# Three norms' reciprocal roots moved behind the projections, and RWKV's fills and transpositions moved, in a two-block hybrid kernel

## What is computed

```python
def rms_norm_2(x, g):
    y = xf * lax.rsqrt(jnp.mean(xf * xf, axis=-1, keepdims=True) + RMS_EPS)
    return (y * g.astype(jnp.float32)).astype(x.dtype)

def swiglu(h, w_gate, w_up, w_down):
    return (jax.nn.silu(h @ w_gate) * (h @ w_up)) @ w_down

h = h + 0.5 * swiglu(rms_norm_2(h, ffn1_norm), ffn1_w_gate, ffn1_w_up, ffn1_w_down)   # d_ff 2816
proj = rms_norm_2(h, mix_norm) @ w_in
sb_out = stick_breaking_attention(q, k, v)     # from the first 1536 columns of proj
rw_out = rwkv7_time_mix(proj[..., 1536:], ...) # shift, decays, a recurrence, group norm
h = h + concat([sb_out, rw_out]) @ w_out
h = h + 0.5 * swiglu(rms_norm_2(h, ffn2_norm), ffn2_w_gate, ffn2_w_up, ffn2_w_down)
out = rms_norm_2(h, final_norm)[:, 16:]
```

## Time and profile before

| | |
|---|---|
| median of 3 runs | 1085.91 us (1084.17 to 1086.17) |
| profiled execution | 1086.47 us, its span 1084.7 us |
| PE busy | 1000.6 us, 92% of the span |
| weight loads (PEld) | 952.5 us, 88% |
| DVE busy | 533.3 us, 49% |
| ACT busy | 535.3 us, 49% |
| POOL busy | 654.5 us, 60% |
| DMA | 139.79 MB, mean 129 GB/s |
| mean granted PE clock | 0.965 of 2.4 GHz |

### The profile page before, as it was taken

The page is one execution under the profiler, slowest core; times in us unless marked ns, Lnnn a source line. Parts: engine busy times, 40 slices in busy tenths (PEclk is TensorE's granted clock), DMA queues, the critical chain, the costliest instruction groups (busy, mean ns, idle before and its releaser), DMA issues.

```text
span 1084.7 us, 22914 instructions
## 1 busy us (share of the span) xinstructions
PE 1000.6 (92%) x9068; PEld 952.5 (88%) x9068; DVE 533.3 (49%) x735; ACT 535.3 (49%) x765; POOL 654.5 (60%) x271
## 2 busy tenths in 40 slices
PE   5997999898799778999999999999999989999996
PEld 5986778697799766899999998999898979999996
DVE  4335433554410895586652003474363668777301
ACT  5565555466554445644444446666321454444441
POOL 2784233356689830698787875554620169888882
PEclk8998999989899899999999999999898999999999
DMA  8552122133355200455555554333200036555551
GB/s 320 191 167 87 61 75 94 63 126 124 127 187 174 79 1 1 140 191 175 179 170 176 173 175 136 117 117 98 98 4 2 21 135 195 194 185 182 188 181 41
DMA packets 38993, 139.79 MB, mean 129 GB/s; under 512 B 4224, under 2 KB 5504, under 8 KB 38784
## 3 DMA queue, kind: packets, MB, share of 16 engines
q1 hardware_dynamic: 38912, 138.62, 37.8%
HBM read 137.55 MB, written 1.05 MB: 128 GB/s over the span
## 4 chain that ended last, share of the span: by engine, by line
PE 55%; issue 22%; POOL 12%; DVE 8%; ACT 2%; DMA 1%; SPq 0%; POOLq 0%; DVEq 0%; ACTq 0%
PE ps L667 55%; POOL wlo L602 11%; DVE qkl L1834 3%; DVE hA L2133 1%; DVE hT L1866 1%; ACT whi L1463 1%; ACT dif L1402 1%; DMA ring<-in_stream 1%; DVE sq L1834 0%; ACT rstd L1402 0%; PE ps L1208 0%; POOL dif L626 0%; DVE hA L1834 0%; DVE rGI L1834 0%; DVE aL L1872 0%
## 5 line engine op out<-in xcount | busy, mean ns | idle before, releaser
L602 POOL TENSOR_TENSOR wlo<-ring,whi 128x1024 fp32r<-128x1024 f32 x251 | 611.5, 2453 | 381.4 <-ACT whi L1463 380.3
L667 PE MATMUL ps<-aH,whi 128*128 128x256 f32 (+1 forms) x1528 | 445.4, 291 | 27.1 <-DVE aL L1834 10.3
L667 PE MATMUL ps<-aH,wlo 128*128 128x256 f32 (+1 forms) x1528 | 439.7, 288 | 0.0
L667 PE MATMUL ps<-aL,whi 128*128 128x256 f32 (+1 forms) x1528 | 439.5, 288 | 0.0
L1463 ACT ACTIVATE whi<-ring 128x1024 fp32r<-128x1024 f32 x253 | 266.4, 1058 | 123.7 <-PE ps L667 108.0
L667 PEld LDWEIGHTS ps<-aH,whi 128*128 128x128 f32 x1528 | 294.8, 193 | 35.8 <-issue 17.7
L667 PEld LDWEIGHTS ps<-aH,wlo 128*128 128x128 f32 x1528 | 294.8, 193 | 0.0
L667 PEld LDWEIGHTS ps<-aL,whi 128*128 128x128 f32 x1528 | 294.2, 193 | 0.3 <-issue 0.2
L667 PE MATMUL ps<-fH,wlo 128*128 128x272 f32 (+1 forms) x352 | 100.8, 286 | 0.0
L667 PE MATMUL ps<-fH,whi 128*128 128x272 f32 (+1 forms) x352 | 100.4, 285 | 0.0
L667 PE MATMUL ps<-fL,whi 128*128 128x272 f32 (+1 forms) x352 | 100.4, 285 | 0.0
(11 more groups left out here) (336 smaller groups left out, 1303.4 us busy)
## 6 DMA issues: line engine op xcount, KB each, us to landing
ring<-in_stream SPq DMA_DIRECT2D x253, 512.0 KB, 3.3
cst<-in_cst SPq DMA_DIRECT2D x1, 1325.0 KB, 13.4
xT<-in_x SPq DMA_DIRECT2D x4, 272.0 KB, 3.5
out<-hT SPq DMA_DIRECT2D x1, 1024.0 KB, 4.6
row<-in_row SPq DMA_DIRECT2D x1, 898.0 KB, 9.9
cst<-in_cst SPq DMA_DIRECT2D x1, 640.0 KB, 10.9
mat<-in_mat SPq DMA_DIRECT2D x1, 576.0 KB, 14.2
vec<-in_vec SPq DMA_DIRECT2D x1, 135.0 KB, 3.8
```

Source lines behind the costliest of these rows:

```text
L602: nc.gpsimd.tensor_tensor(wlo[:, s, :], ring[:, s, :], whi[:, s, :].bitcast(F32), ALU.subtract).then_inc(S("w_split"), 1)
L667: return nc.tensor.matmul(out, lhsT, rhs, start=start, stop=stop, skip_group_check=True)
```

## The change

**Norms of ffn1, mix and ffn2 (`LATE`).** The activations of the next projection are now `xT` times the gain, without `rstd`: as soon as a tile of `xT` is there, ACT writes the high part and the square, and DVE the low part (`low_half`), within `residual`. For the FFNs they lie in `fxH` and `fxL`, which share the memory of `hT` and `mixT`. PE starts the projection's first pair and only behind it makes the norm sum, one matmul, for which DVE adds all eight squares. No filler stands at these norms any more, and the copy of the last weight ahead is made before `rstd` on ACT. `rstd` is applied behind the projection: in the FFN, DVE multiplies the gate's bank in place and ACT's tanh waits for that (`ffn_gate`); the up half needs it also, so the result of the down projection is multiplied in `residual` (tags mix and final). In the mixer, DVE multiplies each RWKV tile in place ahead of ACT's shift (`mix_scaled`) and drains q, k and v itself with the multiply in the same step (before: ACT).

**RWKV.** POOL's `inverse_starts` now comes before the `wlo` of the first four units of the output projection, which follow it. The key transpositions, four before at one place behind the ladder, now stand one behind the last level, two ahead of the second group's last products, one where it was, in other banks.

```diff
+LATE = ("ffn1", "mix", "ffn2")
+SUMMED = {n: 8 if n in LATE else 5 for n in NORMS}
...
-            lows(U_HO + SLOTS, U_PO + SLOTS)
+            lows(U_HO + SLOTS, U_PO)
             inverse_starts()
-            lows(U_PO + SLOTS, N_UNITS)
+            lows(U_PO, N_UNITS)
...
             def norm(tag, n):                                       # PE
-                else:
+                elif tag not in LATE:
                     filler(1)
-                pe.wait_ge(S("norm_sum"), (SUMMED - 1) * (i + 1))
-                mm(ps[:, 7, 0:n], C("ones"), sq[:, 0, 0:n], True, False)
+                pe.wait_ge(S("norm_sum"), sums_up_to(tag))
+                m = mm(ps[:, 7, 0:n], C("ones"), sq[:, 0, 0:n], True, SUMMED[tag] == KT)
...
-                if i and tag != "final":
+                if tag == "norm1":
                     filler(3)
...
-                feature_pair(u0, g0, c0, ("norm_h", NORMS.index(tag) * KT))
+                feature_pair(u0, g0, c0, ("norm_h", NORMS.index(tag) * KT), tag)
+                norm(tag, TT - c0)
...
-                pe.wait_ge(S("drained_a"), drained("a", G_P + 11 + 3 * m))
+                pe.wait_ge(S("drained_v"), drained("v", G_P + 11 + 3 * m))
...
+                turned(6, key(0, 0)).then_inc(S("r_tok"), 1)
                 pe.wait_ge(S("r_wc"), 3)
                 for g, b in ((0, 0), (1, 4)):
                     pe.wait_ge(S("r_g"), level_count(last_level(g), g))
+                    if g == 1:
+                        turned(2, key(0, 1)).then_inc(S("r_tok"), 1)
+                        turned(3, key(1, 0)).then_inc(S("r_tok"), 1)
...
-                turned(2, key(0, 0)).then_inc(S("r_tok"), 1)
-                turned(3, key(0, 1)).then_inc(S("r_tok"), 1)
-                turned(6, key(1, 0)).then_inc(S("r_tok"), 1)
                 pe.wait_ge(S("r_tokb"), 1)
-                turned(2, key(1, 1)).then_inc(S("r_tok"), 1)
+                turned(6, key(1, 1)).then_inc(S("r_tok"), 1)
...
+                if tag in LATE:                                      # ACT, square()
+                    func(acts(tag)[0][:, k, c0:TT], xT[:, k, c0:TT], ACT.Identity, "norm_hi", scale=V(tag, k))
                 func(sq[:, k, 0:n], xT[:, k, c0:c0 + n], ACT.Square, "norm_sq")
...
+                if tag in LATE:                                      # ACT, squares_behind()
+                    ahead(u0 + n_units - 1)
                 norm(tag, n)
-                ahead(u0 + n_units - 1)
+                if tag not in LATE:
+                    ahead(u0 + n_units - 1)
...
-                    act.wait_ge(S("w_used"), it * 8 + (u0 + 2 * f4 + 1))
+                    act.wait_ge(S("ffn_gate"), it * 4 + (first + f4 + 1))
...
             def residual(tag, g0, c0, scale=1.0):                    # DVE
+                for m in range(KT + 1):
+                    if m < KT:
+                        dve.wait_ge(S("w_used"), used_by(g0 + m))
+                        if tag in ("mix", "final"):
+                            tt(out, out, rstd[:, 0:TT - c0], ALU.mult)
+                        stt(xT[:, m, c0:TT], out, scale, xT[:, m, c0:TT], ALU.mult, ALU.add, "drained_v")
+                    if tag in LATE and m >= 1:
+                        low_half(tag, m - 1, wide)
+                if tag in LATE:
+                    for k in range(1, SUMMED[tag]):
+                        add_square(tag, k, wide)
+                    dve.wait_ge(S("norm_rstd"), NORMS.index(tag) + 1)
+
+            def low_half(tag, k, n):
+                high, low = [t[:, k, TT - n:TT] for t in acts(tag)]
+                dve.wait_ge(S("norm_hi"), NORMS.index(tag) * KT + k + 1)
+                stt(low, xT[:, k, TT - n:TT], V(tag, k), high.bitcast(F32), ALU.mult, ALU.subtract, "norm_h")
...
+                    gate = ps[:, (g0 + 2 * f4) % MM_BANKS, 0:TT - c0]   # DVE, pair()
+                    dve.wait_ge(S("w_used"), it * 8 + (u0 + 2 * f4 + 1))
+                    nc.vector.tensor_tensor(gate, gate, rstd[:, 0:TT - c0], ALU.mult).then_inc(S("ffn_gate"), 1)
                     dve.wait_ge(S("ffn_th"), it * 4 + (first + f4 + 1))
...
+                    if i is None:                                    # DVE, mixer_in()
+                        kind, m = P_STICK[j]
+                        stt(stick[kind][:, m, 0:TT], now, 0.125 if kind == "q" else 1.0, rstd[:], ALU.mult, ALU.mult, "drained_v")
+                    else:
+                        tt(now, now, rstd[:], ALU.mult, "mix_scaled")
                         dve.wait_ge(S("shift"), n_shift + 1)
...
-            norm("ffn1", 0, TT, "ffn1")
             ffn(U_F1, G_F1, 0, 0)
-            norm("mix", 0, TT, "mix")
```

More of the change, by code:

```diff
@@ L77 @@
 P_STICK = [None] * 10 + [(n, j) for j in range(4) for n in "qkv"] + [None] * 4
-P_OWNER = "".join("a" if t is None else "v" for t in P_RWKV)
+P_OWNER = "v" * 26
 P_Z = {12: 0, 15: 1, 18: 2, 21: 3}
@@ L91 @@
 MM_BANKS = 4
-SUMMED = 5
 def chunk_bank(c):
@@ L360, with sums_up_to @@
 NORMS = ("norm0", "norm1", "ffn1", "mix", "ffn2", "final")
+LATE = ("ffn1", "mix", "ffn2")
+SUMMED = {n: 8 if n in LATE else 5 for n in NORMS}
+def sums_up_to(tag):
+    return sum(SUMMED[n] - 1 for n in NORMS[:NORMS.index(tag) + 1])
 def used_by(g):
@@ L407, in program @@
         xT = sb("xT", [P, KT, TT])
-        hT = sb("hT", [P, KT, TT])
-        mixT = sb("mixT", [P, KT, TT])
+        own = ExitStack()
+        hT = sb("hT", [P, KT, TT], at=own)
+        mixT = sb("mixT", [P, KT, TT], at=own)
+        own.close()
+        fxH = sb("fxH", [P, KT, TT], F32R)
+        fxL = sb("fxL", [P, KT, TT], F32R)
         sq = sb("sq", [P, KT, TT])
@@ L539, in program, with acts @@
         mx.close()
+        def acts(tag):
+            return (fxH[:], fxL[:]) if tag in ("ffn1", "ffn2") else (aH[:], aL[:])
         def V(name, i=0):
@@ L1085, in mixer_in @@
                 feature_pair(U_P, G_P, 0, ("norm_h", 3 * KT))
+                norm("mix", TT)
                 for j in range(2, P_UNITS):
@@ L1415, in norm @@
                 func(rstd[:, 0:n], rstd[:, 0:n], ACT.Exp, "norm_rstd", scale=-0.5)
-                if tag != "final":
+                if tag in ("norm0", "norm1"):
                     for k in range(KT):
@@ L1723, in mixer_in @@
                            14: decay_products, 15: decay_quotients, 17: decay_inverses}
-                stick = {"q": sbq, "k": sbk, "v": sbv}
                 n_shift = 0
                 for j in range(P_UNITS):
-                    act.wait_ge(S("w_used"), used_by(G_P + j))
                     now = ps[:, (G_P + j) % MM_BANKS, 0:TT]
-                    if P_RWKV[j] is None:
-                        kind, m = P_STICK[j]
-                        func(stick[kind][:, m, 0:TT], now, ACT.Copy, "drained_a", scale=0.125 if kind == "q" else 1.0)
-                    else:
+                    if P_RWKV[j] is not None:
+                        act.wait_ge(S("mix_scaled"), n_shift + 1)
                         if n_shift == 0:
@@ L1853, in norm @@
                 if tag == "norm0":
-                    for k in range(1, SUMMED):
+                    for k in range(1, SUMMED[tag]):
                         add_square(tag, k, n)
@@ L2080, in residual @@
             def residual(tag, g0, c0, scale=1.0):
[L2081 to L2087 removed]
+                wide = TT if tag in ("ffn1", "mix") else T
+                for m in range(KT + 1):
+                    if m < KT:
+                        dve.wait_ge(S("w_used"), used_by(g0 + m))
+                        out = ps[:, (g0 + m // 2) % MM_BANKS, (m % 2) * T:(m % 2 + 1) * T] if tag in ("norm1", "ffn2") else \
+                            ps[:, (g0 + m) % MM_BANKS, 0:TT - c0]
+                        if tag in ("mix", "final"):
[3 more added lines that the diff above has]
+                        low_half(tag, m - 1, wide)
+                    if tag not in LATE and 2 <= m <= SUMMED[tag]:
+                        add_square(tag, m - 1, wide)
+                if tag in LATE:
+                    for k in range(1, SUMMED[tag]):
+                        add_square(tag, k, wide)
[4 more added lines that the diff above has]
+                stt(low, xT[:, k, TT - n:TT], V(tag, k), high.bitcast(F32), ALU.mult, ALU.subtract, "norm_h")
             def hgrn_in():
@@ L2172, in pair @@
                     nc.vector.scalar_tensor_tensor(out=half, in0=fth[:, f4, c0:TT], scalar=1.0,
-                                                   in1=ps[:, (g0 + 2 * f4) % MM_BANKS, 0:TT - c0], op0=ALU.add,
+                                                   in1=gate, op0=ALU.add,
                                                    op1=ALU.mult).then_inc(S("drained_v"), 1)
@@ L2259, in mixer_in @@
                 step(nc.vector.memset(pS[:, :, 0:1], 0.0), "sb_pad")
+                stick = {"q": sbq, "k": sbk, "v": sbv}
                 n_shift = 0
@@ L2381, in _ @@
             residual("ffn2", G_PO, TM)
-            norm("ffn2", TM, T, "ffn2")
             ffn(U_F2, G_F2, FT, TM)
```

31 lines of the change are left out of this document (12 added, 19 removed).

## The result

| | before | after |
|---|---|---|
| median, measured side by side | 1086.03 us (1084.17 to 1086.17) | 1154.32 us (1153.54 to 1155.38) |
| ratio | | 1.0628, 95% interval 1.0600 to 1.0656 |
| profiled execution, its span | 1086.47, 1084.7 us | 1153.73, 1151.9 us |
| mean granted PE clock | 0.965 | 0.958 |

The account below looks back on a forecast made before the run. PE, busy 92%, was taken as the bound, replaced in FFN pairs by a wait loop. FFN1 28.7, FFN2 37.5, mixer 3.3, RWKV -1.4, final norm 0.5: +68.6 on 1086.47, or 1155.1; median 1154.5, range 1118 to 1167.

Parts of the forecast that it names:

- The ring in the FFN pairs: FFN1, FFN2: tanh waits for the multiply behind the previous pair's `fL`, itself held by `wlo`; 7.25 and 7.19 us, +34.3 and +40.7.
- rival (A): FFN pairs: DVE's cast gets the port before POOL, loop 5.4 us, under PE's pace; 1076 us, faster; chance 0.11.
- The give-back: End of each FFN block: first down tile's addition comes sooner after the last tanh; 4.4 us in FFN1, 3.9 in FFN2.
- FFN1's norm: Ahead of FFN1: PE goes straight on, then idles 2.2 us for the sum; first tanh -1.2 us (-3.5 to +1.2).
- FFN2's: Norm ahead of FFN2: four low halves held behind five `wlo`, sum late; first tanh +0.7 us (-2 to +3).
- The mixer: Mixer with late norm: decay matmuls 0.5 us sooner, then a wait for k; +3.3 us in all (-0.5 to +4).
- the wait for k: Mixer: PE waits for k of head pair 0, its drain queued behind `keys()` on DVE; 3.8 us, or 0.
- RWKV: RWKV part: fills and transpositions gain, `late(2)` behind four `wlo` loses; -1.4 us in all (-10 to +5).
- the fills: RWKV: PE's 2.44 us wait for POOL's fills goes, with some half-clock time behind it; -4.1 us.
- the ladder's loss: RWKV ladder: `late(2)` on DVE stands behind four back-to-back `wlo`; +4.7 us, and +2 for clock lost by idle PE.
- (B): FFN pairs: the loop forms but some pairs escape, each saving 1.2 to 1.9 us; half escaping gives 1119 us; chance 0.06.
- (D): DVE late in more places: all seven additions blocked per norm, PE at half clock behind idle; 1162 us, within main case's 0.80.

## Why the prediction was right, point by point

**The ring in the FFN pairs** held as described: 7.19 us a step for 272 columns (7.25 foretold) and 7.13 for 256 (7.19), casts of 2.37 and 2.36, `fL` of 2.42 and 2.41. Undoing its order or its hold gives 65 us back. The 2 us per block that I had too much are, in FFN1, rival (A) in one pair (2.5) and 0.06 a step (1.2), against 1.7 more for the loop's returns. The table loads at these returns are there: 478.82 to 487.72 is 8.90, which is 1.7 over a plain step where I took 1.28. The other 0.4 is DVE's: its multiply came 0.55 us behind `fL` at the return (at 485.87) and 0.12 elsewhere. The lead that I thought decided, 0.27 us, was smaller in the steady ring (0.15), and POOL kept it. Rival (A)'s step, which I put at 5.4 us, took 4.73 and 4.64.

**The give-back** was 2.9 and 2.8, not 4.4 and 3.9. I let PE have only nine matmuls left behind the last `fL`. But the last tanh came 2.5 us early, so that PE had its own down tile to do, from 611.77 on, and was the later one.

**FFN1's norm**: PE did go straight on and waited 2.03 us for the sum (2.2 foretold). Still the tanh came 0.2 later, not 1.2 earlier; within the bounds, but not by the steps that I named. None of the seven additions was held; the last two low halves ahead of them were, for 2.6 us each:

```profile
444.77 5.20 DVE L1860 SCALAR_TENSOR_TENSOR fxL<-xT,vec,fxH 128x272 fp32r<-128x272 f32 x2
449.89 3.29 DVE L1851 TENSOR_TENSOR sq<-sq 128x272 f32<-128x272 f32 x7
```

PE's pair itself began 0.76 us late, behind a `wlo`, and the way from the sum to tanh took 4.05 us where I had 3.4. **FFN2's**: +1.4 against +0.7. Five of eight low halves took 1.5 to 2.3 us beside POOL, where I had four, and one of the seven additions was held for 2.62, so that they took 5.37 together.

**The mixer** is the step that was wrong: +9.6 against +3.3, outside its bounds (-0.5 to +4). Entry -0.5 and the wait for k of 4.2 (3.8) were right. I had counted PE's waits there at their length and nothing for the clock behind them, though I had done so in RWKV, from the earlier trace rows. By the lengths of the stretches 5.4 of the 9.6 us are half clock: 2.7 before the first logits (7.4 more, less 4.2 and 0.55 of waiting), 2.7 behind them, where no wait was added. The granted clock agrees: 17.1 us of the stretch stand at the half level in the changed kernel, 3.4 in the one before. The run with filler bears it out.

**RWKV**: -6.4 against -1.4, within the bounds. The signs and places were right. In the changed kernel the fills were worth 5.7 (4.1), the spreading 5.7 (4), the ladder's loss 5.0 (6.7): more half clock went with the two waits than I had allowed. **Final norm** -0.5 against +0.5.

The time itself, 1154.3 against 1154.5, owes something to luck: the mixer's 6 us too little stand against RWKV's 5 and the ring's 4 too much, and the give-backs' 2.6 and the norms' 2.1 too little against 2.3 of drift ahead of the change and 1 at the final norm. Of the rivals, (A) lives in 2 pairs of 44; (B) asked for half of them. (D) was right in kind, PE's clock behind its idle time, but in the mixer; in the pairs the clock did fall (0.95 over 465 to 600 us, where it was 1.00), but the ring hid it: PE waited for POOL in every round anyway.

## What to carry to other kernels

Before a step is put in front of an engine that was free to run ahead, write down who waits for whom until the line meets itself; if it does, the ring's length is the pace, whatever each engine's busy share. Here a step of 0.45 us cost 65, and the same step two places earlier in its queue cost nothing that can be told. An idle piece of PE is priced at its length and, where the work behind it is thin, at what the clock takes after it; where the wait was left in place, filler was worth about 3 us. And a drain queued behind long SBUF steps is not mended by moving it one place: ask what the engine has to do in the whole stretch.

## What the runs showed of the hardware

- A cast and a subtraction of 128x272 with SBUF inputs take 0.44 us alone and 2.4 behind a `wlo`; with the input in PSUM they take 0.44 inside one.
- Who holds the port is decided by very little: by the starts in the profile, 0.04 us ahead of the `wlo` the cast took 0.30; 0.15 behind, 2.39.
- PE's granted clock stood at 0.93 over the mixer with idle pieces of 1.9, 2.4 and 3.8 us, and at 1.00 with filler in them and 0.5, 1.3 and 0.9 us left (a fourth piece, of 1.7, was there in both). The price is not fixed: the changed kernel's wait of 3.49 us was followed by 10.3 us at the half level; a wait of the same length at the same place, in the kernel with `keys()` moved, was followed by 3.4 us.
- A load of the tanh table takes 1.28 us and stands at each return of the counted loop. It is hidden while ACT runs ahead; in the ring it is on the way.
- The part of the program ahead of every edit ended at 440.5 to 449.3 us in fourteen traced executions, though nothing in it was edited. Two traces are best compared from a landmark just ahead of the change.
